# A transformer block in fp32 on one core: two of the weight sums of a block product move from VectorE to an accumulating DMA, for three of eight quads

## The reference, cut to what matters

```
u = rmsnorm(h, norm_ff_pre[l])                               # (256, 2048)
f = jnp.square(jax.nn.relu(u @ w_ff1[l])) @ w_ff2[l]         # (256, 8192) @ (8192, 2048)
h = h + rmsnorm(f, norm_ff_post[l])
```

## Time and profile before

| | us |
|---|---|
| median of 3 runs | 1319.78 (1319.35 to 1320.92) |
| the profiled execution | 1320.38 |
| its span | 1318.6 |
| PE busy | 1307.8 (99%) |
| PE weight loads busy | 1118.0 (85%) |
| DVE busy | 923.9 (70%) |
| ACT busy | 668.3 (51%) |
| POOL busy | 47.0 (4%) |

### The profile page before, as it was taken

The page is one execution under the profiler, slowest core; times in us unless marked ns, Lnnn a source line. Parts: engine busy times, 40 slices in busy tenths (PEclk is TensorE's granted clock), DMA queues, the critical chain, the costliest instruction groups (busy, mean ns, idle before and its releaser), DMA issues.

```text
span 1318.6 us, 18299 instructions
## 1 busy us (share of the span) xinstructions
PE 1307.8 (99%) x6998; PEld 1118.0 (85%) x6998; DVE 923.9 (70%) x1265; ACT 668.3 (51%) x922; POOL 47.0 (4%) x92
## 2 busy tenths in 40 slices
PE   9999999999999999999999999999999999999998
PEld 8889989888888888888988888887888878888886
DVE  7765565687875555547868866589876899676554
ACT  7554454465664444454645665445454464445442
POOL 1222110000000000000000000000000000000000
PEclk9999999999999999999999999999999999999999
DMA  9766555555566666774774656746477464776663
GB/s 301 220 182 170 164 161 163 156 166 159 169 191 191 189 192 205 229 244 154 239 255 161 236 185 189 236 151 213 151 222 238 142 208 160 234 251 188 225 194 105
DMA packets 135498, 256.75 MB, mean 195 GB/s; under 512 B 8308, under 2 KB 45584, under 8 KB 134781
## 3 DMA queue, kind: packets, MB, share of 16 engines
q1 hardware_dynamic: 131360, 243.50, 58.4%
q0 software_dynamic: 2160, 4.74, 1.7%
q10 hardware_dynamic: 1900, 7.46, 1.6%
HBM read 251.39 MB, written 4.27 MB: 194 GB/s over the span
## 4 chain that ended last, share of the span: by engine, by line
PE 93%; DVE 3%; DMA 2%; issue 0%; ACT 0%; SPq 0%; ACTq 0%
PE bank L2041 17%; PE bank L1731 11%; PE bank L1733 11%; PE bank L1732 11%; PE bank L2044 9%; PE bank L2091 5%; PE bank L2092 5%; PE bank L2093 5%; PE bank L1777 4%; PE bank L1765 3%; PE bank L1766 3%; PE bank L1764 3%; PE bank L1779 2%; DMA s_raw<-in_w_ff 1%; PE bank L2065 1%; DVE b_lo L1570 1%
## 5 line engine op out<-in xcount | busy, mean ns | idle before, releaser
L1050 DVE TENSOR_TENSOR w_lo<-raw,w_hi 128x1024 fp32r<-128x1024 f32 (+1 forms) x360 | 429.9, 1210 | 248.2 <-ACT w_hi L586 246.8
L586 ACT ACTIVATE w_hi<-raw 128x1024 fp32r<-128x1024 f32 (+1 forms) x360 | 371.2, 1047 | 295.3 <-DMA raw<-in_w_ff 173.2
L2041 PE MATMUL bank<-f_hl,w_hi 128*128 128x512 f32 x960 | 229.7, 391 | 0.0
L2041 PEld LDWEIGHTS bank<-f_hl,w_hi 128*128 128x128 f32 x960 | 176.4, 188 | 34.1
L2044 PEld LDWEIGHTS bank<-f_hl,w_lo 128*128 128x128 f32 x960 | 123.1, 191 | 4.7
L2044 PE MATMUL bank<-f_hl,w_lo 128*128 128x256 f32 x960 | 124.5, 283 | 0.0
L1731 PE MATMUL bank<-w_hi,u_hl 128*128 128x512 f32 x256 | 101.1, 395 | 0.0
L1733 PE MATMUL bank<-w_hi,u_hl 128*128 128x512 f32 x256 | 99.9, 390 | 0.0
L1732 PE MATMUL bank<-w_lo,u_hl 128*128 128x512 f32 x256 | 99.8, 390 | 0.0
L906 ACT ACTIVATE s_hi<-s_raw 128x1024 fp32r<-128x1024 f32 x48 | 50.7, 1055 | 75.3 <-DMA s_raw<-in_w_ff 75.3
L1765 PE MATMUL bank<-u_hl,w_lo 128*128 128x272 f32 x288 | 82.4, 289 | 0.0
(11 more groups left out here) (282 smaller groups left out, 2311.1 us busy)
## 6 DMA issues: line engine op xcount, KB each, us to landing
raw<-in_w_ff SPq DMA_DIRECT2D x160, 512.0 KB, 4.1
raw<-in_w_in SPq DMA_DIRECT2D x128, 512.0 KB, 3.7
s_raw<-in_w_ff SPq DMA_DIRECT2D x48, 512.0 KB, 3.9
b_raw<-in_w_ff SPq DMA_DIRECT2D x24, 1024.0 KB, 5.2
raw<-in_w_out SPq DMA_DIRECT2D x32, 512.0 KB, 4.5
raw<-in_w_branch_b SPq DMA_DIRECT2D x16, 512.0 KB, 3.8
raw<-in_w_branch_a SPq DMA_DIRECT2D x16, 512.0 KB, 3.8
xt<-in_turned_x SPq DMA_DIRECT2D x8, 272.0 KB, 5.6
```

What stands on the lines that cost most here:

```text
L586: act.activation(w_hi[:, u, :, 0:width], raw[:, u, :, 0:width], ACT.Copy).then_inc(hi_ready, 1)
L1050: dve.tensor_tensor(w_lo[:, u, :, 0:width], raw[:, u, :, 0:width], w_hi[:, u, :, 0:width].bitcast(F32), ALU.subtract).then_inc(lo_ready, 1)
L2041: ins = pe.matmul(acc[g][:], w_hi[:, u, k, cols], f_hl[:, kt, :], start=kt == 0, stop=kt == KT - 1)
```

## The change

The sums get other signs, so that two of the four are plain additions that a DMA can do: pieces 3 and 4 become (3 + 1) and (3 + 2) in place of (1 - 3) and (3 - 2). The hidden sums (`activate_hidden`) and the last additions (`join`) change their signs to match, with the same number of instructions and the same shapes. For the quads n = 3, 4 and 5 of the quarters 0, 1 and 2:

- SP issues a second DMA behind the 1 MB load, which copies piece 3 from the memory once more, into place 4 (256 KB, `b_copied`).
- POOL waits for both and issues an accumulating DMA from SBUF to SBUF, pieces 3 and 4 += pieces 1 and 2 (512 KB, `b_added`).
- DVE's `sum` falls away; in its place in the list stands a wait for `b_added`.

For the other quads DVE does `sum` as before, with an addition. Cut to its core:

```diff
+BY_DMA = (3,4,5)
...
                 sp.dma_start(b_raw[i][:, 0:4, :]...).then_inc(b_landed[i], 16)
+                if k in BY_DMA:
+                    sp.dma_start(b_raw[i][:, 4, :], w_ff2[0, bass.ds(q * D + (4 * j + 1) * P, P), slice(c * 1024 + CW, c * 1024 + 1024)])\
+                      .then_inc(b_copied[i], 16)
...
+            for q in range(QUARTERS - 1):
+                for k in BY_DMA:
+                    i = B_SLOT[k]
+                    pool.wait_ge(b_landed[i], b_lands(q, k, 16))
+                    pool.wait_ge(b_copied[i], b_sums(q, k))
+                    pool.dma_start(b_raw[i][:, 3:5, :], b_raw[i][:, 1:3, :], accum_op=ALU.add).then_inc(b_added[i], 16)
...
-                if kind == "sum":
+                if kind == "sum" and n in BY_DMA:
+                    dve.wait_ge(b_added[i], b_sums(q, n))
+                    dve.sem_inc(b_part, 1)
+                elif kind == "sum":
                     dve.wait_ge(b_landed[i], b_lands(q, n, 16))
-                    dve.tensor_tensor(raw_b[:, 4:2:-1, :], raw_b[:, 3:0:-2, :], raw_b[:, 2:4, :], ALU.subtract)\
+                    dve.tensor_tensor(raw_b[:, 4:2:-1, :], raw_b[:, 3:0:-2, :], raw_b[:, 2:4, :], ALU.add)\
                        .then_inc(b_part, 1)
...
-                ins = dve.tensor_tensor(dst, dst, other, ALU.add).then_inc(p_part, 1)
+                dve.tensor_tensor(dst, one, other, ALU.subtract if step in (4, 6) else ALU.add).then_inc(p_part, 1)
```

More of the change, by code:

```diff
@@ L332, in hybrid_block @@
         b_landed = [sem(f"b_landed{i}") for i in range(3)]
+        b_copied = [sem(f"b_copied{i}") for i in range(3)]
+        b_added = [sem(f"b_added{i}") for i in range(3)]
         h2_stored, h2_landed = sem("h2_stored"), sem("h2_landed")
@@ L382, in b_lands, with b_sums @@
             return each * (B_BEFORE[n] + 1 + q * B_COUNT[B_SLOT[n]])
+        def b_sums(q, n):
+            mine = [k for k in BY_DMA if B_SLOT[k] == B_SLOT[n]]
+            return 16 * (mine.index(n) + 1 + q * len(mine))
         def hi_no(q, kind, n):
@@ L1514, in activate_hidden @@
                 dve.wait_ge(hid_part, n + 1)
-                dve.tensor_tensor(work[:, 8, :], work[:, 3, :], work[:, 1, :], ALU.add).then_inc(hid_part, 1)
+                dve.tensor_tensor(work[:, 8, :], work[:, 3, :], work[:, 1, :], ALU.subtract).then_inc(hid_part, 1)
                 dve.wait_ge(hid_part, n + 2)
@@ L1519, in activate_hidden @@
                 dve.wait_ge(hid_part, n + 3)
-                dve.tensor_tensor(work[:, 10, :], work[:, 0, :], work[:, 9, :], ALU.subtract).then_inc(hid_ready, 1)
+                dve.tensor_tensor(work[:, 10, :], work[:, 0, :], work[:, 9, :], ALU.add).then_inc(hid_ready, 1)
             def keep_hidden(q, j, last):
@@ L1558, in split_item @@
                     dve.wait_ge(b_part, part + 1)
-                    dve.tensor_tensor(raw_b[:, 5, :], raw_b[:, 1, :], raw_b[:, 4, :], ALU.subtract).then_inc(b_part, 1)
+                    dve.tensor_tensor(raw_b[:, 5, :], raw_b[:, 1, :], raw_b[:, 4, :], ALU.add).then_inc(b_part, 1)
                 elif kind == "sum4":
                     dve.wait_ge(b_part, part + 2)
-                    dve.tensor_tensor(raw_b[:, 6, :], raw_b[:, 0, :], raw_b[:, 5, :], ALU.subtract).then_inc(b_ready, 1)
+                    dve.tensor_tensor(raw_b[:, 6, :], raw_b[:, 0, :], raw_b[:, 5, :], ALU.add).then_inc(b_ready, 1)
                 elif kind == "first":
@@ L1599, in join @@
                                       for b in range(BLOCKS) for h in range(2)]
-                dst, other = ((c11, p1), (p6, p1), (p7, p6), (c21, p7), (p6, p5), (c12, p6), (p7, p5), (c22, p7))[step]
+                dst, one, other = ((c11, c11, p1), (p6, p6, p1), (p7, p7, p6), (c21, c21, p7), (p6, p5, p6), (c12, c12, p6),
+                                   (p7, p5, p7), (c22, c22, p7))[step]
                 if step:
                     dve.wait_ge(p_part, step)
-                ins = dve.tensor_tensor(dst, dst, other, ALU.add).then_inc(p_part, 1)
+                dve.tensor_tensor(dst, one, other, ALU.subtract if step in (4, 6) else ALU.add).then_inc(p_part, 1)
                 if step == 7:
```

## The result

The changed kernel takes 1334.12 us (median of 6 runs, 1331.14 to 1337.2) against 1319.89 us before (6 runs, 1319.35 to 1321.06). The ratio is 1.0106, 95% interval 1.0089 to 1.0123: slower by 14 us. Forecast were 1323.1 us with a range to 1330.0. The sign was right, the size was a quarter of what came.

What follows compares the result with a forecast made beforehand. PE was taken as the bound. Lateness from quad 4's and 5's waits, less what `add_x` stops swallow, summed to 3 L - 13.15 = +3.35 us at L = 5.5, so 1323.1 us, range 1317.6 to 1330.0.

Steps and rivals of the forecast that it cites:

- What bounds the kernel, and the most that can be won: PE, busy 1307.8 of 1318.6 us; six stops in the second stages allow at most 4.6 us, 0.35% of the span.
- L: Time from POOL's issue of the accumulating DMA to its landing; estimated 4.3 to 7.0 us, taken as 5.5.
- small handover: Step from the copy's landing to POOL's issue, left inside L without a size of its own.
- The rule of the Trainium skill that I weighed: Accumulating DMA takes 2.0 us plus bytes at 436 GB/s, about 3.2 us; faster, 1316.9 us; chance 0.10.
- A stop costs its idle time and 0.26 us: Each PE stop in the second stages costs its idle time plus 0.26 us; six stops together 4.6 us.
- In quarter 2 the same pattern: Quad 4's wait in quarter 2 makes DVE later by L - 3.90, as in quarter 1.
- the sharing of the DMA engines: S loads slowed by the accumulation on shared DMA engines: costed at nothing beside L, bounded at 3 us for quad 4.
- One stop at quad 3: PE stops at `rest` 3 for about 1.9, 2.7 and 2.1 us in place of 0.34, 0.64 and 0.51.
- The copy delays S5 by 0.75 us: In SP's queue the extra 256 KB make S5's load land 0.75 us later.
- `add_x` swallows 0.94 us in two quarters: In quarters 1 and 2 PE's second stop, for `add_x` (0.68 + 0.26 us), partly absorbs the lateness.
- The stop of quad 2 in quarter 1 goes: PE's stop at 900.37, 0.20 us idle behind quad 2's `rest`, disappears, worth 0.46 us.
- Quad 5 adds little: Quad 5's wait adds nothing in quarter 0; L - 4.97 against L - 4.84 in quarter 1, L - 4.37 decides quarter 2.

Runs made afterwards that it cites:

- dve_late: Kernel before, no DMA added, DVE held up behind S5 by 8 useless additions in each quarter; 1335.23 us, ratio 1.011.
- dve_late_short: Kernel before, no DMA added, DVE held up behind S5 by 5 useless additions in each quarter; 1330.59 us, ratio 1.0068.
- later: Changed kernel, DVE's wait and sums of the next quad moved behind `first`, `rest` and the next S item of the quad before; 1322.11 us, ratio 1.0008.
- copy_only: Changed kernel with the 256 KB copies but no accumulating DMA, DVE making all sums itself; 1323.87 us, ratio 1.0024.
- late_wait: Changed kernel, same DMAs, DVE's wait and sums of the next quad moved behind `first` and `rest` of the quad before; 1324.75 us, ratio 1.0027.
- only4: Changed kernel with only quad 4 summed by DMA, not quads 3 and 5; 1328.17 us, ratio 1.0059.
- later_copy: As later, but SP issues the 256 KB copy behind the next S load, not ahead of it; 1323.55 us, ratio 1.0021.
- signs: Changed kernel with no quad given to the DMA, so only the signs differ from the kernel before; 1321.39 us, ratio 1.0004.

## Why the prediction was wrong in size

The three stages grew by 15.7 us in the profiled execution, and my sum had 3.35. Of the 12.4 us between them, 5.9 are matmuls at the lower clock, a term that the sum did not have, and 6.5 are lateness of DVE, which cost PE 9.8 us (11.7 less twice 0.94) and not 3.35. Of these 6.5, 0.6 lie in quarter 0.

- **What bounds the kernel, and the most that can be won: right.** No version won more than 0.13%, and DVE's 9.6 us bought nothing by themselves.
- **L, in no row before, taken as 5.5 us: right in quarter 0, too small for quad 4 in the other two (7.5 and 6.7).** In quarter 0 quad 4's accumulation landed 5.3 us after its issue. A term I had left inside L came out bigger than a "small handover": the copy was issued at 721.89 and landed after 6.8, at 728.7; POOL issued at 729.28, 0.6 us later, and DVE began 0.2 after the landing. From copy to `first` 3 it was 6.1 us. 6.1 - 3.94 = 2.2, measured 2.14. The rule of the Trainium skill that I weighed (page "DMA: Bandwidth & Descriptors", section "Anatomy of one DMA — SWDGE (gpsimd) path", an estimated 3.2 us) does not agree with any of the nine landings, 4.4 to 7.5.
- **"A stop costs its idle time and 0.26 us": this step failed.** It held for the short stops of before. In the changed kernel the two stops of a quarter, 2.4 to 5.1 us of idle time together, brought the clock down to 1.2 GHz, in quarter 2 the first of them by itself, and 5.9 us went there, in a term that my sum did not have. dve_late shows the same without any DMA, dve_late_short its price, 2.85 us in one quarter.
- **"In quarter 2 the same pattern", and quarter 1 by the landings of before: this step failed too.** The forecast for `rest` 3 there was 1.6 us late; it came 5.28 and 4.29 late. Of the 3.7 us beyond the forecast in quarter 1, 2.0 are the accumulation (7.5 us in place of 5.5), 1.0 the copy's landing and 0.7 the handovers to POOL and to DVE; the 2.7 of quarter 2 are 1.2, 0.7 and 0.8. The copy landed late because the load of quad 4 was issued 17.87 us after the stage's start in place of 16.72: an S load and with it the split that SP waits for came late (DVE idled 1.91 us for S2, whose load took 5.4 and not 4.3 us). I had named the sharing of the DMA engines as a cost of zero. It is not: the load of quad 5 took 6.8, 8.1 and 7.5 us in the changed kernel in place of 5.1 to 5.2, and 10.0 in later; in copy_only, with the copy and no accumulation, it took 5.2 to 5.3. And how long quad 4's accumulation takes goes with how close it lies to that 1 MB load, in the five runs that have it:

  | the load of quad 5 is issued | accumulations of quad 4 | they took, us |
  |---|---|---|
  | 1.07 to 1.54 us after POOL's issue | 7 (after 0; late_wait 0; later 0, 2; only4 0, 1, 2) | 5.1 to 5.6 |
  | 0.55 to 0.93 us after | 4 (after 1, 2; late_wait 1, 2) | 6.4 to 7.5 |
  | 0.20 us after to 0.87 us before | 4 (later 1; later_copy 0, 1, 2) | 9.5 to 10.9 |

  (The digits are the quarters, "after" is the changed kernel.) By these rows a late load of quad 4 is paid twice, once as it is and once because its accumulation moves toward the next load. later_copy moved it there and got the long times in all three quarters; no run moved the distance alone. The DMAs of quad 3 are not needed for an explanation: quarter 0 of the changed kernel has them, and 5.3 us.
- **One stop at quad 3: incomplete.** I followed `rest` 3 and not `first` 3. When both are late PE stops twice, once for 0.60 to 3.33 and once for 1.24 to 1.79 us. For the lateness this changes nothing; for the clock it may, since in quarter 0 neither stop by itself (0.60 and 1.79 us) was of a length that always brought it down.
- **The copy delays S5 by 0.75 us: right.** S5's load took 6.7 in place of 6.04 us in quarter 0; copy_only cost 3.2 us (2.5 against signs), a little above 3 x 0.75.
- **`add_x` swallows 0.94 us in two quarters: right.** Both stops are gone.
- **The stop of quad 2 in quarter 1 goes: right, and useless,** another of 0.60 us for S2 came near it.
- **Quad 5 adds little: right only beside quad 4.** Alone it costs 4.6 us, by a stop for `add_p` that was on no path of mine.

## What to carry to other kernels

Moving a step from an engine that is not the bound to a DMA replaced 1.2 us of work by 6 us of latency here, and in an in-order list the place of the wait decides more than the work saved: the same DMAs cost 14 us with the wait ahead of the urgent instructions and 1 us behind them (2.8 us against the same order without them). Before trading work for a DMA, try the order alone; here it was all of the gain. Look also at what the new DMA lies beside: the same accumulation took 5 to 6 us with more than 1 us of lead on a 1 MB load and about 10 us when issued together with it. And price a new stall on TensorE with its clock: in these runs a stop from about 1.8 us on often brought it down, and each fall cost 1.5 to 2.9 us more for the matmuls behind it.

## What the runs showed of the hardware that was not expected

- An accumulating DMA of 512 KB from SBUF to SBUF, fp32, took 4.4 to 7.5 us in the changed kernel, and 10.9 us when a 1 MB load was issued 0.2 us after it, which itself took 10.0 in place of 5.2 us. POOL was occupied 0.84 to 0.89 us by the issue, against 0.55 for a plain one of 136 KB.
- Stops of PE of nearly the same length (0.76 and 1.78, and 0.96 and 1.78 us, 2.7 us apart) were followed by the lower clock in one quarter and not in the next of the same execution (dve_late_short). Single stops of 3.33, 2.67, 2.51, 2.32 and 1.85 us were all followed by it.
